# Attention scores from one full-precision product to three single-rate products on each head's own rows, issued in bundles over two or three heads

## What is computed

```python
# NSA, selected and window branch: 8 heads of 64 each, over the same keys of the head's group
s_w = jnp.einsum('bcqgrd,bckgd->bcgrqk', qb, kb).astype(f32) * scale
# layers: differential attention, two components of 32 rows per head
sc = jnp.einsum('bhcqd,bhckd->bhcqk', qi, k).astype(jnp.float32) * scale
p = jax.nn.softmax(sc, axis=-1)
a = p[:, :, 0] - lam * p[:, :, 1]
# layers: plain (moba) and dilated heads of 64 rows: softmax(q k) v
```

## Time and profile before

| | |
|---|---|
| time, median of 3 runs | 2214.19 us (2212.74 to 2214.22) |
| profiled execution, its own time | 2214.59 us |
| its span in the trace | 2212.8 us |
| TensorE busy | 2160.8 us (98%) |
| VectorE busy | 1500.5 us (68%) |
| ScalarE busy | 944.2 us (43%) |
| GpSimd busy | 1189.3 us (54%) |
| mean granted clock of TensorE | 0.995 |

### The profile page before, as it was taken

How to read it: one execution, slowest core, us unless ns; L and a number is a source line. 1 busy time by engine, 2 the same in 40 slices (tenths; PEclk the granted TensorE clock), 3 DMA queues, 4 the chain that set the end, 5 groups by cost and what they waited for, 6 DMA issues and landing times.

```text
span 2212.8 us, 33023 instructions
## 1 busy us (share of the span) xinstructions
PE 2160.8 (98%) x12331; PEld 1840.0 (83%) x12331; DVE 1500.5 (68%) x2224; ACT 944.2 (43%) x1882; POOL 1189.3 (54%) x582
## 2 busy tenths in 40 slices
PE   6999999999999999999999999999999999999997
PEld 4788888877899988887887898888897887888885
DVE  6834877554666692897646776677896728777676
ACT  3254663011556610644743555412555725455311
POOL 4747403776477677745016644577653037444673
PEclk9999999999999999999999999999999999999999
DMA  8422102422133333232002222322221012222221
GB/s 318 156 73 86 62 30 88 181 94 96 58 115 115 109 142 135 77 115 77 1 4 92 96 91 100 115 95 84 107 93 61 1 39 86 92 90 115 95 95 57
DMA packets 32776, 206.78 MB, mean 93 GB/s; under 512 B 4080, under 2 KB 4336, under 8 KB 11632
## 3 DMA queue, kind: packets, MB, share of 16 engines
q1 hardware_dynamic: 32192, 200.27, 24.9%
q10 hardware_dynamic: 432, 4.46, 0.5%
HBM read 202.61 MB, written 2.10 MB: 93 GB/s over the span
## 4 chain that ended last, share of the span: by engine, by line
PE 87%; DVE 8%; DMA 1%; DVEq 1%; issue 1%; ACT 1%; POOL 1%; POOLq 0%; SPq 0%; ACTq 0%
PE PS L1118 18%; PE PS L1120 18%; PE PS L1119 18%; PE PS L1560 5%; PE PS L1572 5%; PE PS L1375 3%; PE PS L1373 3%; PE PS L1374 3%; PE PS L1586 3%; PE PS L1449 2%; PE PS L1451 2%; PE PS L1450 2%; DMA raw<-slabs_dram 1%; DVE PS L3374 1%; PE PS L1132 1%
## 5 line engine op out<-in xcount | busy, mean ns | idle before, releaser
L665 POOL TENSOR_TENSOR w_hi<-raw,zero_c 128x512 fp32r<-128x512 f32 (+1 forms) x135 | 279.5, 2088 | 546.2 <-PE PS L1120 544.8
L669 POOL TENSOR_TENSOR w_lo<-raw,w_hi 128x512 fp32r<-128x512 f32 (+1 forms) x135 | 367.4, 2740 | 5.8
L1118 PE MATMUL PS<-b_hi,w_hi 128*128 128x512 f32 x528 | 209.8, 397 | 1.0 <-POOL w_lo L888 1.0
L1119 PE MATMUL PS<-b_lo,w_hi 128*128 128x512 f32 x528 | 209.3, 396 | 0.0
L1120 PE MATMUL PS<-b_hi,w_lo 128*128 128x512 f32 x528 | 209.3, 396 | 0.0
L3288 DVE TENSOR_TENSOR b_lo<-a_all,b_hi 128x512 fp32r<-128x512 f32 x44 | 162.5, 3732 | 49.4 <-ACT b_hi L2446 49.4
L1118 PE MATMUL PS<-f_hi,w_hi 128*128 128x512 f32 x448 | 177.6, 397 | 0.7 <-DVE f_lo L2590 0.7
L1120 PE MATMUL PS<-f_hi,w_lo 128*128 128x512 f32 x448 | 177.6, 396 | 0.0
L1119 PE MATMUL PS<-f_lo,w_hi 128*128 128x512 f32 x448 | 177.6, 396 | 0.0
L688 POOL TENSOR_TENSOR w_lo<-raw,w_hi 128x512 fp32r<-128x512 f32 x48 | 71.0, 1479 | 93.6 <-ACT w_hi L2438 93.6
L1118 PEld LDWEIGHTS PS<-b_hi,w_hi 128*128 128x128 f32 x528 | 99.5, 188 | 25.6 <-POOL w_lo L888 1.2
(11 more groups left out here) (570 smaller groups left out, 6822.3 us busy)
## 6 DMA issues: line engine op xcount, KB each, us to landing
raw<-slabs_dram SPq DMA_DIRECT2D x161, 1024.0 KB, 4.8
aux<-ada_dram SPq DMA_DIRECT2D x18, 512.0 KB, 5.0
ada_first<-ada_dram SPq DMA_DIRECT2D x11, 512.0 KB, 13.9
cmpw<-cmpw_dram ACTq DMA_DIRECT2D x2, 2048.0 KB, 11.7
ada_late<-ada_dram SPq DMA_DIRECT2D x8, 512.0 KB, 3.3
ada_last<-ada_dram SPq DMA_DIRECT2D x8, 512.0 KB, 5.8
xT<-xT_dram SPq DMA_DIRECT2D x1, 2048.0 KB, 9.2
out_dram<-t SPq DMA_DIRECT2D x4, 512.0 KB, 2.7
```

Source lines behind the costliest of these rows:

```text
L665: high = nc.gpsimd.tensor_tensor(w_hi[:, slot, c], raw[:, slot, c], zero[:, 0:c.stop - c.start], ALU.add)
L669: low = nc.gpsimd.tensor_tensor(w_lo[:, slot, c], raw[:, slot, c], w_hi[:, slot, c].bitcast(f32), ALU.subtract)
L1118: nc.tensor.matmul(out, a_hi_, b_hi_, start=start, stop=False)
L1119: nc.tensor.matmul(out, a_hi_, b_lo_, start=False, stop=False)
```

## The change

1. **Three products for a score.** Queries and keys of NSA and of the layers are kept as a high and a low part of type fp32r. A score becomes three accumulating products (L1611 of the changed kernel): high by high, high by low, low by high. MLA's scores stay as they were.
2. **Own rows.** The zero-filled copies go. A product takes only the rows of its head: 64 for NSA, plain and dilated heads, 32 for a component of a differential head (`rows`).
3. **At least 256 columns.** `wide = max(2, nb)`: where a score has 128 keys, the product covers 256.
4. **Bundles.** Scores are issued `together`: in NSA and for the dilated heads two heads (`mate`), one on rows 0 to 63 and one on rows 64 to 127, for the same tile j; in the first half of the layers three, component 0, component 1 and a plain head on the other half of the rows. A bundle issues its first products, then its second, then its third ones, and only then goes on. It waits once, ahead of its first product, for the banks of all its scores.
5. **Turns split.** Each turn now has a high part on ScalarE and a low part on VectorE, which subtracts the high part from the bank and so waits for ScalarE.
6. Order of jobs and homes of the outputs follow: mates share an output bank, and both are finished after the second's last value product. Some tiles move in SBUF.

```diff
+                    group = [m + 1, m] if woven else [m, m + 1] if jobs[m]["mate"] else [m]
...
+                        if jobs[m]["mate"] or woven:
+                            self.together[at0] = tuple(range(at0, len(self.scores)))
...
+                    for i in plan.together.get(step, ()):
+                        m = plan.scores[i][0]
...
+                        if i >= s_banks:
+                            pe.wait_ge(scores_masked, g0 + i - s_banks + 1)
...
+                    elif step in plan.together:
+                        for part, (of_q, of_k) in enumerate(((0, 0), (0, 1), (1, 0))):
+                            for i in plan.together[step]:
+                                m, c, j, _ = plan.scores[i]
+                                lo, nb = key_range(jobs[m], j)
+                                rows_, wide = jobs[m]["rows"][c], max(2, nb)
+                                last = nc.tensor.matmul(PS[:, i % s_banks, 0:128 * wide],
+                                                        key_tiles(jobs[m]["q"][c][of_q], rows_, j, 1),
+                                                        key_tiles(jobs[m]["k"][of_k], rows_, lo, wide),
+                                                        start=part == 0, stop=part == 2)
+                                if part == 2:
+                                    last.then_inc(scores_ready, 1)
...
-                        nc.tensor.matmul(PS[:, step % s_banks, 0:128 * nb], query_tile(jobs[m]["q"][c], j),
-                                         jobs[m]["k"][:, 128 * lo:128 * (lo + nb)], start=True, stop=True
-                                         ).then_inc(scores_ready, 1)
...
+        def split_turn(src, homes, scale):
+
+            hi, lo = homes
+            return (src, P, [(hi, scale)], [(lo, hi, scale)])
...
+                            m = plan.values[v][0]
+                            for m in plan.finishes[plan.values[v][0]]:
+                                finish(jobs[m], m, plan.sums[m][0] % 8, plan.home[m])
...
                 def two_taken(n):
                     _, _, _, dves = two_turns[n]
-                    if dves:
-                        dve.wait_ge(turned, turn0 + n + 1)
-                    for dst, scale in dves:
-                        V.tensor_scalar(dst, laid(PS[:, n % 4 if n < HEAD else 3, :], dst), scale, None, ALU.mult
-                                        ).then_inc(turned_dve, 1)
+                    dve.wait_ge(turned_act, act0 + counts[n][0])
+                    for dst, hi, scale in dves:
+                        V.scalar_tensor_tensor(out=dst, in0=laid(PS[:, n % 4 if n < HEAD else 3, :], dst), scalar=scale,
+                                               in1=laid(hi.bitcast(f32), dst), op0=ALU.mult, op1=ALU.subtract
+                                               ).then_inc(turned_dve, 1)
```

More of the change, by code:

```diff
@@ L1041, in build @@
-            two_jobs.append(job((diff_q[2 * h], diff_q[2 * h + 1]), T2b[:, 2 + h // 2, :],
+            other = h + 1 - 2 * (h % 2)
+            two_jobs.append(job((plain_q[other // 2],), plain_k[other // 2],
+                                lambda kb, h=other: z2[:, 2, kb, 256 + 64 * h:320 + 64 * h],
+                                O2[:, :, 512 + 64 * other:576 + 64 * other], causal, vector=False,
+                                rows=(half_rows(other),)))
+            two_jobs.append(job((diff_q[h // 2], diff_q[h // 2]), diff_k[h // 2],
@@ L1042, in build @@
                                 lambda kb, h=h: z2[:, 1, kb, 64 * h:64 * h + 64],
-                                O2[:, :, 768 + 64 * h:832 + 64 * h], causal, vector=False))
+                                O2[:, :, 768 + 64 * h:832 + 64 * h], causal, vector=False,
+                                rows=tuple(slice(64 * (h % 2) + DIFF * c, 64 * (h % 2) + DIFF * c + DIFF)
+                                           for c in (0, 1))))
         for h in range(8):
-            two_jobs.append(job(dilated_q[h], T2a[:, h // 2, :],
+            two_jobs.append(job((dilated_q[h // 2],), dilated_k[h // 2],
@@ L1052, in build @@
         o2_step = {step: n for n, (step, _, _) in enumerate(O2_TURNS)}
[L1055 to L1062, removed]
+        def split_turn(src, homes, scale):
+            hi, lo = homes
+            return (src, P, [(hi, scale)], [(lo, hi, scale)])
         def laid(bank, dst):
-            return bank.rearrange("p (t d) -> p t d", t=TT) if len(dst.shape) == 3 else bank
+            return bank.rearrange("p (t d) -> p t d", t=TT) if len(dst.shape) == 3 and len(bank.shape) == 2 else bank
         def turned_counts(items):
@@ L1551, in attend @@
+                    if step in plan.together and jobs[plan.scores[step][0]]["rows"] is None:
                         m, c, j, _ = plan.scores[step]
                         lo, nb = key_range(jobs[m], j)
-                        if banks_ready:
-                            banks_ready(step)
-                        if jobs[m]["turned_by"] and step % TT == 0:
-                            pe.wait_ge(mla_act, jobs[m]["turned_by"])
-                            pe.wait_ge(mla_dve, jobs[m]["turned_by"])
```

182 lines of the change are left out of this document (111 added, 71 removed).

## The result

| | before | after |
|---|---|---|
| median of the runs | 2214.2 us (2212.74 to 2215.63, 4 runs) | 2361.5 us (2360.17 to 2368.9, 4 runs) |
| span of the profiled execution | 2212.8 us | 2360.9 us |
| mean granted clock of TensorE | 0.995 | 0.940 |
| PE busy | 98% | 2278.2 us, 96% |
| instructions on PE | 12331 | 12555 |

The ratio is 1.0672, 95% interval 1.0648 to 1.0696. I forecast 2243 us, with 2262 us as the upper end. The change is slower, as forecast, but by 147 us and not by 29.

A forecast was written before the change was run, and what follows sets the result against it. PE, busy 98%, was taken as the bound, with DVE not far behind. First halves +18 us per layer (+36 for two), with part 1 +28, on the profiled 2214.6 gave 2243 us; range 2200 to 2262.

The forecast's parts named there:

- What bounds the kernel: Whole kernel and the three changed stretches: PE busy 98% of the span, 97% or more in the stretches, DVE 67 to 79%.
- Part 1: NSA and dilated scores in two-head bundles: -3.3 us in NSA, -2.4 per dilated layer, together -8 us.
- the visit: Two-head bundles: going to fewer rows costs 0.10 us, coming out 0.15, so 0.25 charged per bundle.
- rival A: Bundles: different row groups really run side by side, loads too; together -13 us, 2201 us; chance 0.22.
- the lock-step: Three-head bundles: PE waits until all masks are done, DVE has no mask until the bundle is through; 62 us against 53.5.
- Part 2: First half of each layer, three-head bundles: bundle taken as 1.4 us, loops sum to 62 us against 53.5 before.
- Part 3: Split turns in each first half: DVE's low part waits for ScalarE, some 10 us per layer; -0.3 ahead of the layer.
- B: Bundles: products run one after another, no overlap at all; in all +64 us, 2278 us; chance 0.13.
- What would show it: Profile after: first halves some 70 us, PE under 80% busy there, waits for masks and ScalarE's high part topping the list.

## Why the prediction was wrong

- **What bounds the kernel** was right before the change: PE, at a clock of 1.00. But I took the clock for a property of the stretch and not of the work in it. No term, no rival and no bound of the range had it fall, though the change swaps 128-row products for 32- and 64-row ones in just those stretches. **This is the step that failed**, worth 76 us net of the 147. The runs put rows in its place: own rows in the untouched order of before cost 300 us (0.50 in the dilated part), all rows in the changed order brought 0.56 up to 0.93, full-row filler brought it up to 0.93 and 1.00. Two smaller misses stand beside it, each told below: the order of the tiles (23 us, no term) and the price of the bundles (46 us on all rows). Even the kernel on all rows, 2285 us, is above the upper end of 2262.
- **Part 1, bundles of two.** I charged 0.67 for six loads plus 0.25 for the visit. At full clock a bundle took 0.72 us at 384 columns and 0.55 at 256 (1183.01 to 1183.73, 1185.27 to 1185.82): three product times plus 0.2. Loads of the two heads go together, so rival A had the better price. The 0.25 for going in and out, read off the products on 62 rows, was about right. The -8 us came out as +31. On all rows the same stretches still were 21 us over before (NSA 103.5 us, the dilated parts 50.1), so two thirds of it are the pairing and the lock-step, and the rest the rows.
- **Part 2, bundles of three.** The lock-step is real: on all rows bundles cost 46 us in all, 18.8 per first half (57.3 to 76.1), where I had some 8.5 for it; but nine products one after another are in that, and a clock of 0.93. The bundle was mis-sized: 2.6 us at 512 columns and 1.9 at 256 at full clock, not 1.4. I had charged half of six changes at 0.12 because the trace showed none between 32 and 64 rows. All of them cost, and 0.2 us each. The Trainium skill (TensorEngine Tiling (Array Packing), Key Properties) says that a change of the tiling mode drains the engine. The timeline agrees: starts 0.43 us apart where a product alone takes 0.23. I weighed that rule and went by half of it; in full at 0.12 it would still have been too low.
- **Part 3, split turns.** Ten us per layer was too much. DVE did wait 13.3 us for eight turns, but PE was busy 93% of the time meanwhile, so little of that can have counted; at full clock, without bundles, the first half was 3.9 us longer than before and putting the low part a step later took 3.4 of them away.
- **No term at all: the order of the tiles.** The forecast prices the tiles that move in SBUF, at nothing, but not that two heads' equal tiles now follow each other. That was 23 us, most of it in NSA, where PE idled 11.3 us instead of 2.7.
- **Rivals.** A's mechanism (side by side) is there for products of equal shape, and did not make the kernel faster: what ran side by side on part of the rows was not enough to hold the clock. B (one after another) was wrong for heads of one shape and right for the plain head beside the components. Its 2278 us was nearest in number and for the wrong reason.
- **What would show it.** I said that PE's busy share in the first half would be under 80%. It was 93%. That line alone should send a reader to the clock, since products that were to take less time filled twice the time. Nor did PE's waits for the masks top the list (8.7 us); DVE's for PE did (44.1 us). Two products did start nearly together, which was A's sign.

Whether a correct kernel could use the 4 us of the split form stays open. It would need products on all rows, so zeros in the other heads' rows of high and low parts alike, with more copies on ScalarE and VectorE and more memory than the change holds. I did not build one: the ceiling is 4 us, before those copies are paid for.

## What to carry to other kernels

Zero rows in a product may not be free to remove; here they were not. Before cutting a matmul to the rows that matter, ask what else in that stretch works the array in full, and read the granted clock of the stretch in the first run afterwards: a busy share near 100% says nothing if the clock is at half. When a bundle mixes shapes, order it by shape; each change between 32 and 64 rows cost here about as much as a product of 512 columns (0.2 us). And moving equal tiles next to each other is a change of its own: it can cost more than what it is meant to allow.

## What was unexpected of the hardware

- Idle time mattered less than rows. The first half on all rows idled for 20 of 76 us at a clock of 0.93; on 32 and 64 rows it was busy 99% at 0.54.
- The same work fell at different times: in the kernel before on own rows layer 0's first half lost the clock after 5.7 us, layer 1's after 60.4. The same kernel's two runs were 40 us apart. What decides between them no run here shows, and the second run has no trace.
- Two products of equal shape on different rows started together, self-loaded weights included (0.11 us for two of 256 columns), and this without a bundle too, three places apart in the list. In the bundles shown, 32 rows beside 64 never did.
- After a fall everything on PE paid, not only the scores: in the first half the value passes of 64 columns went from 0.105 us each to 0.22 (eight from 1080.25 to 1082.01).
